# Sixteen slots instead of eight for expert weights, and a router with one copy of its logits and no transfers of gates and indices

## The chip, the cores and the metric

The kernel runs on one core of a Trainium2 chip. The metric is the device time of one execution in microseconds (us), the median over several runs. TensorE does the matrix products, VectorE (DVE in the rows) and ScalarE (ACT) the elementwise work, GpSimd (POOL) a few helpers and the gathers, SyncE (SP) issues the loads of weights. All data is float32.

## The reference

One token sequence of 512 tokens and 1024 features passes two blocks. The change touches the end of the first block: a mix (two branches and an output product), a router, and a mixture of 16 experts in which each expert chooses its 64 tokens.

```python
def expert_choice_moe(h, w_router, w_gate, w_up, w_down):
    b_, length, _ = h.shape
    cap = EC_CAPACITY_FACTOR * length // N_EXPERTS
    aff = jax.nn.softmax((h @ w_router).astype(jnp.float32), axis=-1)
    gate, idx = lax.top_k(jnp.swapaxes(aff, 1, 2), cap)
    bidx = jnp.arange(b_)[:, None, None]
    xe = h[bidx, idx]
    hid = jax.nn.silu(jnp.einsum("becd,edf->becf", xe, w_gate)) * jnp.einsum("becd,edf->becf", xe, w_up)
    ye = jnp.einsum("becf,efd->becd", hid, w_down) * gate[..., None].astype(h.dtype)
    return jnp.zeros_like(h).at[bidx, idx].add(ye)
```

w_gate, w_up and w_down are 16 matrices of 1024 x 1024 each: 201 MB that are read once. The second block (another attention, a convolution, a feed-forward layer of width 4096) follows and needs the whole result.

## The kernel before, in words

Each engine has its own program, written out by hand in one function per engine (`pe`, `act`, `dve`, `pool`, `sync`), with a nested function for each stage: `mix`, `router`, `experts`, `second` and so on. The order within an engine is the order of the code; between engines there are only semaphores. A first silent pass over all programs numbers the signals, a second one emits the instructions.

**Weights.** `weight_units` lists every weight load in the order in which it is needed. SyncE issues them in this order (L2566 to L2570). The class `Ring` gives each unit a place in a ring of eight slots of 2048 words per partition (`NS = 8`), so 1024 KB a slot. Before a load, SyncE waits until the holder of the slot has been read (`W.before`, `W.free`). It is one queue: a load that waits holds back all later loads. Units of the mix take two slots each. A unit of the experts takes one: two of the eight rows-of-128 of one expert's matrix, `k == 2`. The experts' units come in the order pair p of experts, then gate, up, down, then `kq` 0 to 3, then the two experts `e2`: 24 units a pair, 192 in all.

**Mix and router.** The mix ends with eight output products, ("wo", 0) to ("wo", 7). The router (L711 on TensorE) then does this, each step waiting for the one before: norm on VectorE and ScalarE into `h2T`; logits with `wr`, eight products in two groups of four (L718), which leave partial sums in four bands of 16 rows at rows 0, 32, 64 and 96; VectorE copies the four bands to `mrow` (L2123); TensorE turns them; VectorE adds the bands, softmax follows; TensorE turns the result to one row per expert, `aff`; VectorE draws the top 64 of 512 in eight rounds (L2145 to L2150) and casts the indices to float32, `ifl` (L2152). Meanwhile TensorE turns `h2T` to token rows, ScalarE copies them to `h2k` (L1410) and stores them to the DRAM scratch `h2_scratch` (L1413, called h_scratch in the rows: the h2 store). Then gates `gv` and indices `ifl`, 16 experts x 64 places each, have to come to one row per place for a pair of experts: four small transfers on ScalarE's queue bring them to `gi8` (L1417), TensorE turns them (L738, L739), VectorE copies them to `giT` and `idx` (L2154, L2155). GpSimd gathers the 128 token rows of pair 0 into `xe` (L2534), after `idx` and after the landing of the h2 store.

**Experts.** For each pair TensorE does `pair_product` of gate (L760), the `scatter` of the pair before (L771), `pair_product` of up, the turns of the next gathered rows, the turns of the hidden values, and `pair_product` of down. After each `kq` the two units read are free. VectorE compares `iot`, the numbers 0 to 511, with the indices to build the scatter matrix `PT` (L2189). After pair 7, the last scatter makes the input of the second block.

## Time and profile before

| | us |
|---|---|
| median of 3 runs | 1996.23 (1995.18 to 2000.35) |
| profiled execution | 1997.07 |
| its span, first to last instruction | 1995.8 |
| TensorE busy | 1762.4 (88%) |
| VectorE busy | 806.3 (40%) |
| ScalarE busy | 560.6 (28%) |
| mean DMA rate over the span | 165 GB/s |

The span is cut into stretches: the mix ends at about 722 us, the router runs to about 772, the experts to about 1252, the second block follows. In the rows PE is TensorE's product, PEld its load of the stationary side, POOL GpSimd, SPq, ACTq and POOLq the issue of a transfer. PS is the product memory. "DMA share" is the mean busy share of the 16 DMA engines. A row of the chain gives start, duration and what ran or was waited for. In a timeline the bracket says how long the engine had been idle and who released it. A group xN is N instructions of one form that followed one another, and the time of such a group reaches from its first start to its last end.

### The profile page before, as it was taken

How to read it: one execution, taken by the hardware profiler on the slowest of the kernel's cores; microseconds unless marked ns; L12 is line 12 of the kernel's file. 1: busy time of each engine (PE TensorE's matmuls, PEld its weight loads, DVE VectorE, ACT ScalarE, POOL GpSimd, SP SyncE). 2: the span in 40 equal slices, each digit the busy share in tenths (PEclk: the TensorE clock that was granted, in tenths of full speed). 3: DMA queues.
4: the chain of work that ended last, by engine and by line, in shares of the span. 5: the costliest groups of instructions: out<-in, count | busy, mean ns of one | idle time of the engine just before them, and what ended most of it. 6: DMA issues, size and time to landing. Idle time of an engine off the chain costs nothing.

```text
span 1995.8 us, 20238 instructions
## 1 busy us (share of the span) xinstructions
PE 1762.4 (88%) x8121; PEld 1140.0 (57%) x8121; DVE 806.3 (40%) x1315; ACT 560.6 (28%) x983; POOL 123.1 (6%) x127
## 2 busy tenths in 40 slices
PE   5999899887999875788888888899888899999998
PEld 2656567556778652233323233487545578888786
DVE  2154754467433342011111011428466634444443
ACT  3134543554423230000000000332444342222221
POOL 0002111113000001000000000000100101100010
PEclk9999899888999987999999999999899799999999
DMA  8221201123511415999999999353300113222301
GB/s 300 91 64 48 80 22 64 42 91 121 169 61 73 168 43 220 421 421 421 421 421 422 421 421 420 139 165 87 127 1 1 43 52 118 84 85 88 123 1 43
DMA packets 92448, 329.38 MB, mean 165 GB/s; under 512 B 7492, under 2 KB 22724, under 8 KB 67780
## 3 DMA queue, kind: packets, MB, share of 16 engines
q1 hardware_dynamic: 85408, 315.80, 41.0%
q10 hardware_dynamic: 5604, 8.04, 1.2%
q0 software_dynamic: 1344, 4.25, 0.6%
q8 instruction: 65, 1.06, 0.2%
q14 instruction: 27, 0.22, 0.0%
HBM read 322.82 MB, written 4.19 MB: 164 GB/s over the span
## 4 chain that ended last, share of the span: by engine, by line
PE 67%; DMA 13%; DVE 11%; ACT 5%; issue 3%; ACTq 1%; SPq 0%; DVEq 0%
PE PS L645 20%; PE PS L760 9%; PE PS L991 8%; PE PS L388 7%; DMA ring<-in_w_exp_down_dram 6%; DMA ring<-in_w_exp_gate_dram 6%; PE PS L384 3%; PE PS L519 3%; PE PS L771 3%; PE PS L601 2%; PE PS L826 2%; PE PS L444 1%; PE PS L666 1%; PE PS L941 1%; PE PS L872 1%
## 5 line engine op out<-in xcount | busy, mean ns | idle before, releaser
L760 PE MATMUL PS<-ring,xeT 128*64 128x512 f32 x1024 | 232.0, 604 | 38.7 <-DMA ring<-in_w_exp_gate_dram 36.4
L1703 DVE TENSOR_TENSOR wR<-ring,wR 128x1024 fp32r<-128x1024 f32 (+2 forms) x134 | 151.3, 1130 | 238.0 <-ACT wR L1102 237.8
L1102 ACT CAST wR<-ring 128x1024 fp32r<-128x1024 f32 (+2 forms) x134 | 130.0, 971 | 212.6 <-PE PS L991 128.1
L760 PEld LDWEIGHTS PS<-ring,xeT 128*64 128x64 f32 x1024 | 77.4, 139 | 191.9 <-issue 185.5
L991 PE MATMUL PS<-wR,hR 128*128 128x512 f32 x768 | 177.8, 392 | 8.9 <-DVE tmp L2421 6.9
L645 PE MATMUL PS<-xR,wR 128*128 128x512 f32 x768 | 175.6, 389 | 0.0
L991 PEld LDWEIGHTS PS<-wR,hR 128*128 128x128 f32 x768 | 144.7, 189 | 42.0 <-DVE tmp L2421 9.6
L645 PEld LDWEIGHTS PS<-xR,wR 128*128 128x128 f32 x768 | 144.0, 188 | 30.3 <-issue 0.4
L760 PE MATMUL PS<-ring,hidT 128*64 128x512 f32 x512 | 116.7, 603 | 24.5 <-DMA ring<-in_w_exp_down_dram 18.6
L645 PE MATMUL PS<-hR,wR 128*128 128x512 f32 x528 | 130.0, 404 | 9.2 <-DVE hR L2402 3.7
L645 PEld LDWEIGHTS PS<-hR,wR 128*128 128x128 f32 x528 | 100.6, 192 | 37.4 <-issue 10.5
L645 PE MATMUL PS<-hR1h,wR 128*128 128x512 f32 x320 | 106.7, 405 | 8.3 <-DVE hR1m L2080 7.4
L760 PEld LDWEIGHTS PS<-ring,hidT 128*64 128x64 f32 x512 | 38.3, 138 | 97.7 <-issue 89.9
L1433 ACT ACTIVATE hid<-PS 128x1024 f32<-128x1024 f32 x8 | 8.2, 1024 | 275.4 <-PE PS L760 275.4
L645 PEld LDWEIGHTS PS<-hR1h,wR 128*128 128x128 f32 x320 | 60.8, 190 | 25.5 <-DVE hR1m L2080 7.8
L2175 DVE TENSOR_TENSOR hid<-hid,PS 128x1024 f32<-128x1024 f32 x8 | 9.8, 1220 | 159.4 <-ACT hid L1433 159.4
L2187 DVE TENSOR_SCALAR ye<-PS,giT 128x512 f32<-128x512 f32 x16 | 11.3, 746 | 151.6 <-PE PS L760 151.6
L601 PE MATMUL PS<-Y 128*128 128x64 f32 x448 | 60.1, 292 | 9.0 <-DVE SS L1986 6.7
L601 PEld LDWEIGHTS PS<-Y 128*128 128x128 f32 x448 | 58.4, 209 | 15.3 <-DVE SS L1986 8.4
L388 PE MATMUL PS<-hT,ring 128*128 128x256 f32 (+1 forms) x192 | 63.1, 486 | 2.9 <-DMA ring<-in_w_in_dram 2.9
L388 PE MATMUL PS<-ring,hT 128*128 128x256 f32 x288 | 63.2, 379 | 0.0
L771 PE MATMUL PS<-PT,ye 128*128 128x512 f32 x128 | 59.1, 608 | 2.1 <-DVE PT L2189 2.1
(416 smaller groups left out, 2516.1 us busy)
## 6 DMA issues: line engine op xcount, KB each, us to landing
ring<-in_w_exp_gate_dram SPq DMA_DIRECT2D x64, 1024.0 KB, 13.6
ring<-in_w_exp_up_dram SPq DMA_DIRECT2D x64, 1024.0 KB, 13.6
ring<-in_w_exp_down_dram SPq DMA_DIRECT2D x64, 1024.0 KB, 13.0
ring<-in_w_mod_dram SPq DMA_DIRECT2D x12, 2048.0 KB, 8.0
ring<-in_w_in_dram SPq DMA_DIRECT2D x11, 2048.0 KB, 11.3
ring<-in_w_up_dram SPq DMA_DIRECT2D x8, 2048.0 KB, 9.0
ring<-in_w_down_dram SPq DMA_DIRECT2D x8, 2048.0 KB, 7.9
ring<-in_w_in_dram SPq DMA_DIRECT2D x9, 1024.0 KB, 5.3
```

The costliest lines, as they stand in the source:

```text
L384: return T.transpose(dst, src, ident[0:k, 0:k])
L388: mm = T.matmul(dst, l, r, start=(i == 0), stop=(i == len(pairs) - 1))
L444: mm = T.matmul(b, hT[:, k, 256 + 128 * i:384 + 128 * i], w[:, k, :], start=(k == 0), stop=(k == 7))
L519: T.matmul(b[:, 0:512], wh[k], hT[:, k, 256:768], start=(k == 0), stop=(k == 7))
L601: mm = T.matmul(b[:, 64 * x:64 * x + 64].rearrange("p (b m) -> p b m", m=LEVELS[l]), yy, half, start=True, stop=True)
L645: mm = T.matmul(b, o[s][:, k, :], x(t, k), start=(k == ks[0] and j == 0), stop=(k == ks[-1] and j == 2))
L760: mm = T.matmul(b[es, ns], stat[:, 2 * kq + k, es], W.view(units[e2])[:, k, ns], start=(kq + k == 0), stop=(kq == 3 and k == 1))
L771: T.matmul(b, ye[:, p % 2, 128 * k:128 * k + 128], PT[:, p % 2, :], start=True, stop=True) \
L826: mm = T.matmul(bs[i][:, 0:cs.stop - cs.start], hR2[:, s, kk + k, 128 * i:128 * i + 128], o[t][:, k, :], start=(kk + k + j == 0), stop=(kk ...
L991: mm = T.matmul(down[m], uR[:, r % 2, s, k, 128 * i:128 * i + 128], o[t][:, 0, 512 * q:512 * q + 512], start=(k + j == 0), stop=(k == 3 an ...
L1102: A.copy(parts(wR, chunks, n)[0], W.view(unit)[:, ks, cs]).then_inc(act_hi.sem, act_hi.up(key))
L1703: V.tensor_tensor(lo, W.view(unit)[:, ks, cs], hi.bitcast(F32), ALU.subtract) \
```

## The change

It has three parts.

First, four "rooms" of two slots each are added to the ring: `room0` and `room1` in memory of the mix (free after the last output product), `room2` where `h2k` lies (free when the h2 store has landed), `room3` where `h2T` lies (free after the last turn into `h2k`). Expert units now go round sixteen places. All other units stay in the ring of eight. `iot` moves out of the way of room 3, and its load moves behind the h2 store.

Second, `wr` is widened from 16 to 32 columns, cleared by a memset before its load, so that the logits' partial sums fill all 128 rows, and one copy takes them all.

Third, the four transfers to `gi8` go. TensorE multiplies `gv` and `ifl` directly with every second column of the identity, which selects the even or odd experts and turns in one product; the result lands in the same layout.

```diff
--- before.py
+++ after.py
@@ -84,19 +84,25 @@
 
 
 
-    def __init__(self, tensor, sems, units):
+
+    def __init__(self, tensor, sems, units, more):
         self.tensor, self.sems, self.units = tensor, sems, units
+        self.places = [tensor[:, 2048 * i:2048 * i + 2048] for i in range(NS)] + [place for _, place in more]
         self.number = {u[0]: i for i, u in enumerate(units)}
         self.slots, self.value, self.before, self.free = [], [], [], {}
-        at, count, holder = 0, [0] * NS, [None] * NS
+        at, turn, count, holder = 0, 0, [0] * len(self.places), [None] * NS + [what for what, _ in more]
         whole = self.number["gate"]
         for i, (name, sources, k, n) in enumerate(units):
-            size, top = 1 if k * n <= 2048 and k <= 4 else 2, 4 if 4 <= i < whole else NS
-            at = 0 if at + size > top or i == whole else at
-            if i == whole:
-                holder[4:] = ["scan"] * 4
-            slots = list(range(at, at + size))
-            at += size
+            if k == 2:
+                slots = [(at + turn) % NS if turn < NS else turn]
+                turn = (turn + 1) % len(self.places)
+            else:
+                size, top = 1 if k * n <= 2048 and k <= 4 else 2, 4 if 4 <= i < whole else NS
+                at = 0 if at + size > top or i == whole else at
+                if i == whole:
+                    holder[4:NS] = ["scan"] * 4
+                slots = list(range(at, at + size))
+                at = (at + size) % NS if i > whole else at + size
             count[slots[0]] += 16 * len(sources)
             self.slots.append(slots)
             self.value.append(count[slots[0]])
@@ -107,8 +113,10 @@
     def view(self, name):
         i = self.number[name]
         _, _, k, n = self.units[i]
-        o = self.slots[i][0] * 2048
-        return self.tensor[:, o:o + k * n].rearrange("p (k n) -> p k n", k=k)
+        first = self.slots[i][0]
+        if len(self.slots[i]) == 1:
+            return self.places[first].rearrange("p (k n) -> p k n", k=k)
+        return self.tensor[:, 2048 * first:2048 * first + k * n].rearrange("p (k n) -> p k n", k=k)
 
     def ready(self, name):
         i = self.number[name]
@@ -228,7 +236,8 @@
     xk = Area(nc, KEEP, KEEP + 4096).take("xk", [128, 4, 1024])
     top = Area(nc, KEEP + 4096, HT)
     xT, sq, rinv = top.take("xT", [128, 8, 512]), top.take("sq", [128, 2, 512]), top.take("rinv", [128, 512])
-    uT, wr, iot = hT[:, :, 0:512], hT[:, 0, 512:640].rearrange("p (k n) -> p k n", k=8), hT[:, 1:3, 512:768]
+    uT, wr = hT[:, :, 0:512], hT[:, 0, 512:768].rearrange("p (k n) -> p k n", k=8)
+    iot = Area(nc, HT, HT + 512).take("iot", [128, 2, 256])
 
     m5 = Area(nc, DYN, DYN + 5216)
     xeT, xe = m5.take("xeT", [128, 8, 2, 128]), m5.take("xe", [128, 1024])
@@ -241,7 +250,7 @@
     hid, hidT = m6.take("hid", [128, 8, 128]), m6.take("hidT", [128, 8, 128])
     aff, gv = m6.take("aff", [16, 512]), m6.take("gv", [16, 64])
     iu, ifl = m6.take("iu", [16, 64], U32), m6.take("ifl", [16, 64])
-    gi8, idx = m6.take("gi8", [8, 2, 128]), m6.take("idx", [128, 8], U32)
+    idx = m6.take("idx", [128, 8], U32)
     h2k = Area(nc, KEEP, KEEP + 4096).take("h2k", [128, 4, 1024])
     h2T = hT[:, 0:8, 0:512]
 
@@ -315,7 +324,11 @@
         return PS[:, 512 * b:512 * (b + n)]
 
 
-    W = Ring(ring, [sem(f"w_slot{i}") for i in range(NS)], weight_units(d))
+    rooms = [Area(nc, *ends).take(name, [128, 2, 2048]) for name, ends in
+             (("room0", (DYN + 5216, DYN + 9312)), ("room1", (DYN + 9312, DYN + 13408)), ("room2", (KEEP, KEEP + 4096)),
+              ("room3", (HT + 512, HT + 4608)))]
+    W = Ring(ring, [sem(f"w_slot{i}") for i in range(2 * NS)], weight_units(d),
+             [(what, room[:, i, :]) for what, room in zip(("mixed", "mixed", "h2k", "h2T"), rooms) for i in range(2)])
     signals = {}
 
     def signal(name):
@@ -335,7 +348,7 @@
     act_ffn, dve_ffn, pool_ffn, pe_ffn = (signal(n) for n in ("act_ffn", "dve_ffn", "pool_ffn", "pe_ffn"))
     s_ident, s_rows, s_rows2, s_gb, s_masks = sem("s_ident"), sem("s_rows"), sem("s_rows2"), sem("s_gb"), sem("s_masks")
     s_x, s_rope, s_wr, s_iot, s_x2 = (sem(n) for n in ("s_x", "s_rope", "s_wr", "s_iot", "s_x2"))
-    s_h2, s_gi, s_ga, s_sh, s_k2, s_out = (sem(n) for n in ("s_h2", "s_gi", "s_ga", "s_sh", "s_k2", "s_out"))
+    s_h2, s_ga, s_sh, s_k2, s_out = (sem(n) for n in ("s_h2", "s_ga", "s_sh", "s_k2", "s_out"))
 
 
     def col_chunks(name, unit, n_tiles, tiles_of_unit, nk=8):
@@ -715,7 +728,7 @@
             for k in range(8):
                 r = 32 * (k % 4)
                 T.wait_ge(*act_moe["h2T", k])
-                mm = T.matmul(b[r:r + 16, :], wr[:, k, :], h2T[:, k, :], start=(k < 4), stop=(k >= 4))
+                mm = T.matmul(b[r:r + 32, :], wr[:, k, :], h2T[:, k, :], start=(k < 4), stop=(k >= 4))
             mm.then_inc(pe_moe.sem, pe_moe.up("logit"))
             b = every.take(T, "logitT", dve_moe["logitT"])
             T.wait_ge(*dve_moe["logit"])
@@ -734,9 +747,12 @@
                         mm = turn(b[:, 128 * k:128 * k + 128], h2T[:, 4 * q + k, 128 * i:128 * i + 128])
                     mm.then_inc(pe_moe.sem, pe_moe.up(("h2k", i, q)))
             b = every.take(T, "gi", dve_moe["idx"])
-            T.wait_ge(s_gi, 64)
-            turn(b[:, 0:8], gi8[:, 0, :], 8)
-            turn(b[:, 8:16], gi8[:, 1, :], 8).then_inc(pe_moe.sem, pe_moe.up("gi"))
+            T.wait_ge(*dve_moe["topk"])
+            for n, src in enumerate((gv, ifl)):
+                for e2 in range(2):
+                    mm = T.matmul(b[64 * e2:64 * e2 + 64, 8 * n:8 * n + 8], src, ident[0:16, e2:16:2],
+                                  start=True, stop=True)
+            mm.then_inc(pe_moe.sem, pe_moe.up("gi"))
 
         def experts():
             def expert_in(p):
@@ -1032,7 +1048,9 @@
             pass
         W.free["scan"] = pe_scan["o", 3, 2]
         mix()
+        W.free["mixed"] = pe_mm[("wo", 7), 0]
         router()
+        W.free["h2T"], W.free["h2k"] = pe_moe["h2k", 3, 1], (s_h2, 16)
         experts()
         second()
         select()
@@ -1350,9 +1368,8 @@
                             A.copy(xT[:, k, :], bank(("xT", k))).then_inc(s.sem, s.up(("xT", k)))
                     if br == 0 and t == 7:
                         A.wait_ge(*dve_mix["hR", 7])
-                        A.dma_start(wr, d["w_router"].rearrange("(k p) n -> p k n", p=128)).then_inc(s_wr, 16)
-                        A.dma_start(iot, d["k_iota"].rearrange("(a b) -> a b", a=2).partition_broadcast(128)) \
-                            .then_inc(s_iot, 16)
+                        A.wait_ge(*dve_mix["wr0"])
+                        A.dma_start(wr[:, :, 0:16], d["w_router"].rearrange("(k p) n -> p k n", p=128)).then_inc(s_wr, 16)
                         A.wait_ge(*pe_mm[key, 0])
                         for k in range(4):
                             A.copy(aR[0][:, k], oattT[:, k, :]).then_inc(s.sem, s.up(("a2", k)))
@@ -1411,10 +1428,7 @@
                         .then_inc(s.sem, s.up(("h2k", i, q)))
             A.wait_ge(*s.last)
             A.dma_start(h2d.rearrange("(t p) n -> p t n", p=128), h2k).then_inc(s_h2, 16)
-            A.wait_ge(*dve_moe["topk"])
-            for e2 in range(2):
-                for n, src in enumerate((gv, ifl)):
-                    A.dma_start(gi8[:, n, 64 * e2:64 * e2 + 64], src[e2:16:2, :]).then_inc(s_gi, 16)
+            A.dma_start(iot, d["k_iota"].rearrange("(a b) -> a b", a=2).partition_broadcast(128)).then_inc(s_iot, 16)
 
         def experts():
             s = act_moe
@@ -2087,6 +2101,7 @@
                                            ALU.add).then_inc(s.sem, s.up(("y", t)))
 
             sub_lo(wRg, mix_chunks, 5)
+            V.memset(wr, 0.0).then_inc(s.sem, s.up("wr0"))
             for h in range(2):
                 gate(h)
                 gated(h)
@@ -2119,9 +2134,7 @@
                 V.scalar_tensor_tensor(h2T[:, k, :], xT[:, k, :], AB[:, 0, k:k + 1], rinv, ALU.mult, ALU.mult) \
                     .then_inc(s.sem, s.up(("h2T", k)))
             V.wait_ge(*pe_moe["logit"])
-            for c in range(4):
-                t = V.tensor_copy(mrow[32 * c:32 * c + 16, :], bank("logit")[32 * c:32 * c + 16, 0:512])
-            t.then_inc(s.sem, s.up("logit"))
+            V.tensor_copy(mrow, bank("logit")[:, 0:512]).then_inc(s.sem, s.up("logit"))
             V.wait_ge(*pe_moe["logitT"])
             V.tensor_reduce(lgt, bank("logitT")[:, 0:512].rearrange("p (i c x) -> p i x c", i=4, c=4)[:, :, 0:16, :], AX,
                             ALU.add).then_inc(s.sem, s.up("logitT"))
```

How SyncE's program changes, from the last load of the mix to pair 1. Before, with the semaphore that each group waits for:

```order
L2570 DMA ring<-in_w_out_dram 128x8x512 [waits dve_lo] x2
L2570 DMA ring<-in_w_exp_gate_dram 128x2048 [waits dve_lo] x8
L2570 DMA ring<-in_w_exp_up_dram 128x2048 [waits pe_moe] x8
L2570 DMA ring<-in_w_exp_down_dram 128x2048 [waits pe_moe] x8
L2570 DMA ring<-in_w_exp_gate_dram 128x2048 [waits pe_moe] x8
```

Now (room_174 to room_177 are rooms 0 to 3):

```order
L2583 DMA ring<-in_w_out_dram 128x8x512 [waits dve_lo] x2
L2583 DMA ring<-in_w_exp_gate_dram 128x2048 [waits dve_lo] x8
L2583 DMA room_174<-in_w_exp_up_dram 128x2048 [waits pe_mm] x2
L2583 DMA room_175<-in_w_exp_up_dram 128x2048 [waits pe_mm] x2
L2583 DMA room_176<-in_w_exp_up_dram 128x2048 [waits s_h2] x2
L2583 DMA room_177<-in_w_exp_up_dram 128x2048 [waits pe_moe] x2
L2583 DMA ring<-in_w_exp_down_dram 128x2048 [waits pe_moe] x8
L2583 DMA room_174<-in_w_exp_gate_dram 128x2048 [waits pe_moe] x2
```

The up units of pair 0 no longer wait for the gate products (pe_moe) but for the end of the mix (pe_mm), for the h2 store (s_h2), and for the turns of `h2T`. The down units wait for the gate products instead.

TensorE's program at the end of the router, from the last turns of `h2T` to the first gathered rows. Before:

```order
L384 MATMUL PS<-ident,hT 128x128 [waits dve_moe]
L384 MATMUL PS<-ident,hT 128x128 x3
L384 MATMUL PS<-ident,gi_134 128x8 [waits s_gi,act_moe]
L384 MATMUL PS<-ident,gi_134 128x8
L384 MATMUL PS<-ident,xe 128x128 [waits act_moe,s_ga]
```

Now:

```order
L397 MATMUL PS<-ident,hT 128x128 [waits dve_moe]
L397 MATMUL PS<-ident,hT 128x128 x3
L753 MATMUL PS<-ident,gv 64x8 [waits dve_moe,act_moe]
L753 MATMUL PS<-ident,gv 64x8
L753 MATMUL PS<-ident,ifl 64x8 x2
```

The two turns that waited for transfers (s_gi) have become four products that wait for VectorE's top-k alone (dve_moe).

## Rows read from the trace of the kernel before

**Rows 1.** Busy time by stretch; the first line names the columns.
```profile
core 0: us, PE busy (x) PEld busy (x) DVE busy (x) ACT busy (x) POOL busy (x), PEclk, DMA share, GB/s
723.00:750.00 27.00, 14.21 (x59) 8.02 (x58) 17.54 (x37) 14.53 (x22) 0.00 (x0) 0.81 0.03 11
755.00:778.00 23.00, 8.11 (x26) 3.61 (x28) 5.29 (x14) 2.45 (x3) 5.68 (x11) 0.52 0.17 46
778.00:783.00 5.00, 5.00 (x26) 1.68 (x24) 0.00 (x0) 0.00 (x0) 0.00 (x0) 1.00 0.72 257
783.00:1238.00 455.00, 389.98 (x1677) 141.77 (x1674) 70.16 (x93) 24.30 (x38) 5.63 (x6) 0.99 1.01 421
846.00:907.00 61.00, 52.23 (x228) 18.97 (x224) 9.67 (x13) 3.17 (x5) 0.94 (x1) 1.00 1.01 421
1253.00:1258.00 5.00, 3.75 (x5) 1.32 (x6) 2.12 (x5) 1.24 (x2) 0.00 (x0) 0.70 1.06 381
```

**Rows 2.** Chain that ended last, expert stage (start us, us, what).
```profile
903.74 3.65 PE PS L760 x16
...
1208.38 3.65 PE PS L760 x16
...
1248.54 3.67 PE PS L760 x16
```

**Rows 3.** Who waited for whom, 846 to 1248 us (us in total, times, longest).
```profile
PE PS L760 <- DMA ring<-in_w_exp_gate_dram: 31.3, 23, 2.5
...
PE PS L760 <- DMA ring<-in_w_exp_down_dram: 14.1, 12, 1.5
```

**Rows 4.** Timeline of the router (start us, us, engine line, what, idle before).
```profile
735.20 2.79 DVE L2123 COPY mrow<-PS 16x512 f32<-16x512 f32 x4 [1.88 <-PE PS L718]
...
740.52 0.22 DVE L2138 TENSOR_TENSOR lgt<-lgt,lst 128x64 f32<-128x64 f32 x1
740.86 0.54 PEld L384 LDWEIGHTS PS<-ident,lgt 128*16 128x16 f32 x4 [2.34 <-issue]
...
748.41 0.38 ACTq L1413 DMA_DIRECT2D h_scratch<-h2k  x1
...
760.11 0.18 DVE L2152 CAST ifl<-iu 16x64 f32<-16x64 uint32 x1
```

**Rows 5.** The same view, from the index transfers to the first expert product.
```profile
764.26 0.28 PEld L384 LDWEIGHTS PS<-ident,gi 8*128 8x128 f32 x2 [16.84 <-issue]
...
764.67 0.17 DVE L2154 COPY giT<-PS 128x16 f32<-128x16 f32 x1 [4.38 <-PE PS L384]
...
765.20 1.03 POOL L2534 DMA_INDIRECT xe<-h_scratch,idx  x1 [271.04 <-DVE idx L2155]
...
769.56 1.97 PE L384 MATMUL PS<-ident,xe 128*128 128x128 f32 x8 [4.93 <-DMA xe<-h_scratch,idx]
...
772.21 23.24 PE L760 MATMUL PS<-ring,xeT 128*64 128x512 f32 x96 [0.68 <-ACT xeT L1425]
...
778.33 11.10 SPq L2570 DMA_DIRECT2D ring<-in_w_exp_up_dram  x8
```

**Rows 6.** Line of the copy of a full 128x512 product.
```profile
L1713 DVE COPY mrow<-PS x4: 680/690/692, 24.7 to 36.4; 128x512 f32<-128x512 f32 x4
```

**Rows 7.** Line of the h2 store: landing.
```profile
DMA to landing us min/median/max: 6.4/6.4/6.4
```

**Rows 8.** Line of the gather, 760 to 770 us, the queues idle: landing.
```profile
DMA to landing us min/median/max: 4.3/4.3/4.3
```

**Rows 9.** The same line after 800 us, six gathers beside the weight stream: landing.
```profile
DMA to landing us min/median/max: 8.3/8.5/9.5
```

**Rows 10.** DMA issues on the page: KB each and us to landing.
```profile
ring<-in_w_exp_gate_dram SPq DMA_DIRECT2D x64, 1024.0 KB, 13.6
```

**Rows 11.** Timeline of the vector engine at the head of the mix.
```profile
520.89 1.23 DVE L1703 TENSOR_TENSOR wRg<-ring,wRg 128x1024 fp32r<-128x1024 f32 x1 [5.00 <-ACT wRg L1102]
```

**Rows 12.** Line of a memset of 128x512.
```profile
L1731 DVE MEMSET mrow<- x1: 485/485/485, 1.3 to 1.3; 128x512 f32 x1
```

## The prediction

> **What bounds the kernel now.** The profiled execution took 1997.07 us, 0.84 above the median of the three runs shown; its span is 1995.8. I read three views, in this order. First the busy time by stretch: where are the DMA engines full, and where is TensorE? From 783 to 1238 the DMA share is 1.01 at 421 GB/s, while TensorE is busy for 390 of 455 us. The reader is to see that in the expert stage the share of TensorE (86%) looks high, but the thing that has no gap is the weight stream. From 723 to 750 and from 755 to 778, the router and the first gather, the stream is nearly silent: 11 and 46 GB/s [rows 1]. Second the chain of waits, which says what sets the period of the stage: five pairs of experts from 903.74 to 1208.38, so 60.93 us a pair [rows 2]. A pair is 24 units of 1024 KB [rows 10], 25.17 MB, which need 59.8 us at 421 GB/s; one gather of 512 KB adds 1.2. That is the whole period. TensorE has work for 52.23 us of such a pair [rows 1], and the waits table confirms the order: over six and a half pairs TensorE waited 31.3 + 14.1 = 45.4 us for gate and down weights [rows 3], about 7 a pair. Third the timeline between the mix and the first pair. With eight slots, the eight gate units of pair 0 lie ready before the router starts, and the next unit is not issued until TensorE has freed a slot, at 778.33 [rows 5]. From there 184 units follow without a gap; the last lets TensorE go at 1248.54 [rows 2]. So the end of the stage is the moment the stream resumes plus the bytes still missing at that moment. All later work hangs on it.
>
> **Eight more slots.** They take eight of the 184 units out of the stream after the resumption and put them into the silent stretch. Eight units are 8.39 MB; at 421 GB/s that is 19.9 us. This counts only if all eight are there in time. Four go to the rooms of the mix, free when the last product of the mix is done (723); the first stretch of rows 1 is empty enough: 4.19 MB are 10 us, over by about 735, before the h2 store. The other four are issued in order behind a wait for the landing of the h2 store. That store is issued at 748.41 [rows 4], lands 6.4 later [rows 7], and all of it comes 2.1 earlier (below): 752.7. A burst on an idle queue begins to move late: between 778 and 783 the mean was 257 GB/s [rows 1], 1.29 MB, 3.05 us of full rate, so data began near 779.95, 1.6 after the issue at 778.33. Hence the four rooms fill from 754.3 to 764.3. The stream resumes near 774 (below), so there are 10 us to spare, and all eight count.
>
> Does a later wait give it back? A slot is reused 16 units on instead of 8, so the queue waits less than before at every unit. TensorE would need about 52.2 us of work plus some hand-overs, say 54, a pair: 768 + 8 × 54 = 1200 for the end of the last product, against 1252.2 − 24.0 = 1228.2 for the end that the stream sets (now 1248.54 + 3.67 [rows 2]). The stream still ends last, with 28 us of margin. SP is in order: what stands behind the room loads on it are the later weights alone, which had to wait for slots anyway.
>
> **Router logits in one copy.** Four copies of 16 rows take 2.79 us in all [rows 4]. One copy of 128 x 512 takes 0.69 [rows 6]. The price follows the columns, not the rows, and the chain logits, copy, turns, softmax, top-k has nothing beside it: −2.1 us. The logit products become 32 wide instead of 16; their moving side is the same 512 columns, so nothing. The memset that clears the padding covers 256 columns; 512 take 0.485 [rows 12], so 0.25, and VectorE has 5.00 us idle before its next piece of work there [rows 11]: nothing; without that cover it would cost the 0.25.
>
> **Gates and indices by products.** Now the cast of the indices ends at 760.29 [rows 4], four small transfers follow on the ACT queue, the last issued at 762.47, and TensorE starts at 764.26 [rows 5]: 3.97 us. In their place stands a hand-over from VectorE to TensorE. Such a one took 0.12 (740.74 to 740.86) [rows 4]: −3.85. Two turns of eight rows took 0.41 up to the copy behind them (764.26 to 764.67) [rows 5]; the four products are twice as many: +0.4, between 0 and +0.8. I take −3.4 for this part, −5.5 with the copy. The first gather moves from 765.20 to 759.7.
>
> **The iota load** leaves the mix (it was off the path) and stands behind the h2 store on the ACT queue. It is 256 KB, 0.6 us of the stream's rate; VectorE asks for it only after the first gate product, near 785. Nothing.
>
> **What is late next: the first gather.** It used to run on idle queues, 4.3 us to landing [rows 8]. At 759.7 the second four room loads still have 4.6 us to run. The six later gathers, beside a full stream, took 8.3 to 9.5, median 8.5 [rows 9]. So its cost is between 0 and +4.2. It carries 0.52 MB, 1.25 us at full rate. Were it served only after the rooms, it would be over at 764.3 + 1.25 and a few tenths, 765.9; alone it would land at 764.0. I take +1.4, nearer the low end since its neighbour stops at 764.3, while in rows 9 the stream never stops.
> The Trainium skill (DMA: Bandwidth & Descriptors, Queues, rings and completion order) says that each DMA engine goes round between the queues at packet granularity, and (Issuing engines are not separate DMA queues) that transfers of all issuing engines share the same 16 engines. This speaks against the change: the gather cannot pass the room loads. By that rule it shares half and half while they last, an estimate of one more gather's transfer time, +1.25 us, and the sum would differ by 0.15 us. The loaded gathers of the trace agree in direction (8.5 against 4.3).
>
> **Sum.** From the landing of the gather to the first expert product nothing changes: 769.56 to 772.21 [rows 5]. That product starts 5.5 − 1.4 = 4.1 earlier, at 768.1, and the stream resumes 6.1 after it, as now, at 774.2. The stage ends 19.9 + 4.1 = 24.0 us earlier, and nothing behind it changes: second-block weights use the same slots and get them no later. 1997.07 − 24.0 = 1973.1; from the median, 0.84 lower, 1972.2. This last I forecast. Its own bounds: gather free of charge and products free of charge, 19.9 + 5.9 = 25.8, 1970.4; gather at its full +4.2 and products at +0.8, 19.9 + 0.9 = 20.8, 1975.4.
>
> **Rivals.**
> A, half the rooms fill too late (the h2 store lands late beside the iota load, or the four loads behind it hold the gather back as long as they hold each other). For it: everything behind that one wait is in order on SP. Against: 10 us to spare. Only four units count: 10 + 4.1 gives 1982.1.
> B, TensorE becomes the bound. For it: it is busy 52.23 of 61 us and each product waits for one of another engine. Against: rows 3 name DMA before it, for 7 us a pair. It decides from 57.5 us a pair (1228.2 − 768 over eight); at 59 the last product ends at 768 + 472 = 1240, and the gain is 12.2 us: 1984.0.
> C, slower than before: with up to 16 loads outstanding the stream itself runs slower over the whole stage. The one place in the profile where a full share of DMA moves less is 1253 to 1258, with four large loads queued: 381 GB/s at a share of 1.06 [rows 1]. After the resumption 176 units remain, 184.6 MB: 438.4 us at 421, 484.4 at 381. That is +46.0 against −24.0: 2018.2. It decides from 399 GB/s down. Against it: those loads have rows of 2 KB, the expert loads 8 KB, and they ran at 421 for 455 us with up to eight outstanding.
> D, the change does not do what it says: the stage is paced by both sides together, so a head start is lost again within the first pairs, and only the 4.1 us of the router stay: 1992.1. Against it: no gap in the DMA share.
>
> **How the numbers follow.** The forecast within its own bounds has 0.78; A and what lies between it and the forecast 0.08; B 0.04; D 0.03; C 0.03; the other 0.04 is a gain above 26 us. The range for 8 in 10 takes in the forecast's bounds and about 1.5 us on either side for the spread between runs, and reaches toward A: 1969 to 1979. What this kernel's measurement tells from no change is about 0.3%, 6 us. Faster by more: all but C, D and the tail of B, 0.94. Within 0.3%: D and that tail, 0.03. Slower: C, 0.03.
>
> **What would show it.** In the profile after: a DMA share near 1 for 10 us from 723 and for 10 us from about 754; the first gather issued near 759.7 and landing between 4.3 and 6.5 us later; the first expert product near 768, the next weight issue near 774; the period of the late pairs still 60.9 with TensorE waiting for DMA, but in pairs 0 to 3 hardly at all; the last expert product near 1224.5, and everything behind it shifted as a block. The prediction is wrong if the DMA share has gaps between 780 and 1224, if the early pairs take longer than 57 us though no weight is late, or if the gather lands after 768.

## The result, and the profile after

The changed kernel took 1970.64 us (median of 4 runs, 1966.23 to 1973.28) against 1997.1 for the kernel before: a ratio of 0.9864, 95% interval 0.9839 to 0.9888. The forecast was 1972.2, the range 1969 to 1979. A second series gave 1971.64 against 2001.85, ratio 0.9857 (0.9829 to 0.9884). So the gain between medians was 26.5 us in the first series and 30.2 in the second; the forecast was 24.0.

The profiled execution after took 1966.23, which is 30.8 us less than the one before, more than the medians differ. To see what of this is the change, I measure from two marks that exist in both programs: the first instruction of the router on VectorE, right behind the last product of the mix, and VectorE's first read of the last expert product. The timeline of VectorE before has them here:

```profile
723.04 0.16 DVE L2112 SCALAR_TENSOR_TENSOR AB<-modc,colA 128x8 f32<-128x8 f32 x1
...
1252.31 1.41 DVE L2187 TENSOR_SCALAR ye<-PS,giT 128x512 f32<-128x512 f32 x2 [18.05 <-PE PS L760]
```

The same view after, with the router between them:

```profile
718.78 0.16 DVE L2127 SCALAR_TENSOR_TENSOR AB<-modc,colA 128x8 f32<-128x8 f32 x1
...
731.00 0.69 DVE L2137 COPY mrow<-PS 128x512 f32<-128x512 f32 x1 [1.95 <-PE PS L731]
...
753.80 0.18 DVE L2165 CAST ifl<-iu 16x64 f32<-16x64 uint32 x1
...
1223.54 1.41 DVE L2200 TENSOR_SCALAR ye<-PS,giT 128x512 f32<-128x512 f32 x2 [17.79 <-PE PS L776]
```

Between the marks lie 529.3 us before and 504.8 after: 24.5 less, where 24.0 were forecast. The other 6.4 us lie outside: 4.3 ahead of the first mark and 2.1 behind the second. They come back in the section on the experiments, with what they do to the times of the whole.

The busy time by stretch after the change answers to [rows 1]:

```profile
core 0: us, PE busy (x) PEld busy (x) DVE busy (x) ACT busy (x) POOL busy (x), PEclk, DMA share, GB/s
720.00:730.00 10.00, 5.30 (x16) 1.41 (x16) 5.39 (x8) 8.70 (x12) 0.00 (x0) 0.66 0.95 402
730.00:742.00 12.00, 8.43 (x45) 6.86 (x41) 8.25 (x21) 4.58 (x9) 0.00 (x0) 0.71 0.01 1
742.00:750.00 8.00, 0.00 (x0) 0.00 (x0) 7.64 (x18) 0.16 (x1) 0.00 (x0) 0.60 0.78 295
750.00:762.00 12.00, 0.59 (x8) 0.53 (x8) 4.03 (x11) 0.00 (x0) 4.65 (x10) 0.50 0.98 391
763.00:772.00 9.00, 8.33 (x26) 3.29 (x27) 0.00 (x0) 2.45 (x3) 1.03 (x1) 0.56 0.21 58
772.00:777.00 5.00, 5.00 (x26) 1.68 (x24) 0.00 (x0) 0.00 (x0) 0.00 (x0) 1.00 0.82 297
783.00:1205.00 422.00, 376.21 (x1628) 136.22 (x1624) 69.44 (x93) 22.36 (x36) 5.63 (x6) 1.00 1.01 424
```

From 720 to 730 the stream moves 402 GB/s, where there was nothing: rooms 0 and 1. From 730 to 742 it is silent; then come the h2 store and rooms 2 and 3, until 762. Then the first pair starts, and the stream resumes; from 783 on it has no gap, at 424 GB/s instead of 421.

The end of the router, in the timeline after, answers to [rows 4, 5]:

```profile
754.13 0.38 PE L753 MATMUL PS<-ident,gv 16*64 16x8 f32 x4 [12.69 <-DVE ifl L2165]
...
755.29 1.03 POOL L2547 DMA_INDIRECT xe<-h_scratch,idx  x1 [265.80 <-DVE idx L2168]
...
762.73 1.97 PE L397 MATMUL PS<-ident,xe 128*128 128x128 f32 x8 [8.01 <-DMA xe<-h_scratch,idx]
...
765.38 16.71 PE L776 MATMUL PS<-ring,xeT 128*64 128x512 f32 x64 [0.67 <-ACT xeT L1439]
...
771.83 11.11 SPq L2583 DMA_DIRECT2D ring<-in_w_exp_down_dram  x8
```

VectorE casts the indices until 753.98; the products start 0.15 later. The gather is issued 1.31 after the cast's end, where it was 4.91. But the gathered rows come 7.44 us after the gather's issue, where it was 4.36: the landing took

```profile
DMA to landing us min/median/max: 7.4/7.4/7.4
```

against 4.3 before [rows 8]. The first expert product starts 46.6 us after the first mark (before: 49.2) and the next weight load is issued at 53.1 (before: 55.3).

The chain of waits shows the late pairs still paced by the stream. It follows gate products that waited for a load; the first of them stands in pair 2, and the last down product, 1207.69, no longer waits in the chain:

```profile
877.01 3.65 PE PS L776 x16
...
1179.88 3.65 PE PS L776 x16
...
1207.69 15.76 PE PS L776 x64
```

Five pairs now take 302.87 us, 60.57 a pair, against 60.93 [rows 2]. The waits table from 846 to 1224 us has these rows for TensorE and the weights, 37.4 us in all over 378 us, against 45.4 over 402 [rows 3]:

```profile
PE PS L776 <- DMA room<-in_w_exp_gate_dram: 14.6, 11, 2.2
PE PS L776 <- DMA ring<-in_w_exp_gate_dram: 12.4, 10, 1.6
...
PE PS L776 <- DMA ring<-in_w_exp_down_dram: 5.6, 5, 1.3
...
PE PS L776 <- DMA room<-in_w_exp_down_dram: 4.8, 4, 1.4
```

And a load is now issued about 27 us ahead of its landing instead of 14 [rows 10], since TensorE frees sixteen places:

```profile
ring<-in_w_exp_gate_dram SPq DMA_DIRECT2D x32, 1024.0 KB, 26.9
```

### The profile page after: what moved, and what is told of

The parts are those of the page before. It is cut to its first block, busy times and chain, and to the rows that moved or that the text cites. A ratio compares the mean times of both kernels' runs of the same rounds, so it can differ in the third digit from the quotient of the medians.

```text
span 1964.9 us, 20245 instructions
## 1 busy us (share of the span) xinstructions
PE 1758.2 (89%) x8127; PEld 1137.8 (58%) x8127; DVE 803.8 (41%) x1313; ACT 560.5 (29%) x983; POOL 123.1 (6%) x127
## 4 chain that ended last, share of the span: by engine, by line
PE 71%; DMA 10%; DVE 10%; ACT 5%; issue 3%; ACTq 0%; SPq 0%; DVEq 0%
PE PS L658 21%; PE PS L776 11%; PE PS L1007 9%; PE PS L401 7%; DMA ring<-in_w_exp_gate_dram 4%; DMA room<-in_w_exp_gate_dram 4%; PE PS L397 3%; PE PS L532 3%; PE PS L787 3%; PE PS L614 2%; PE PS L842 2%; PE PS L457 1%; PE PS L679 1%; DMA ring<-in_w_in_dram 1%; PE PS L957 1%
## 5 line engine op out<-in xcount | busy, mean ns | idle before, releaser
L776 PE MATMUL PS<-room,xeT 128*64 128x512 f32 x512 | 115.0, 602 | 14.6 <-DMA room<-in_w_exp_gate_dram 14.6
L776 PE MATMUL PS<-ring,xeT 128*64 128x512 f32 x512 | 116.1, 607 | 13.1 <-DMA ring<-in_w_exp_gate_dram 12.4
L658 PEld LDWEIGHTS PS<-hR,wR 128*128 128x128 f32 x528 | 102.0, 195 | 36.2 <-issue 9.4
L776 PEld LDWEIGHTS PS<-room,xeT 128*64 128x64 f32 x512 | 38.4, 138 | 90.5 <-issue 88.2
L776 PEld LDWEIGHTS PS<-ring,xeT 128*64 128x64 f32 x512 | 38.1, 139 | 90.0 <-issue 85.9
L776 PE MATMUL PS<-room,hidT 128*64 128x512 f32 x256 | 58.5, 610 | 7.7 <-DMA room<-in_w_exp_down_dram 4.8
L776 PE MATMUL PS<-ring,hidT 128*64 128x512 f32 x256 | 56.9, 595 | 8.6 <-DMA ring<-in_w_exp_down_dram 5.6
## 6 DMA issues: line engine op xcount, KB each, us to landing
room<-in_w_exp_up_dram SPq DMA_DIRECT2D x32, 1024.0 KB, 26.5
```

Source lines behind the costliest of these rows:

```text
L658: mm = T.matmul(b, o[s][:, k, :], x(t, k), start=(k == ks[0] and j == 0), stop=(k == ks[-1] and j == 2))
L776: mm = T.matmul(b[es, ns], stat[:, 2 * kq + k, es], W.view(units[e2])[:, k, ns], start=(kq + k == 0), stop=(kq == 3 and k == 1))
```

## The experiments

Eleven variants were run, and the changed kernel a second time. All times in this table come from the timeline of each one's profile, counted from the first mark. "First product" is the first expert product, "next load" the first weight load issued after it, "last product" the second mark, "behind" the rest of the span. GB/s is the mean of 800 to 1190 us. Each row is one profile. The two profiles of the changed kernel differ by 1.3 us at the next load and by 1.5 at the last product, but only by 0.2 in the stretch between the two; differences of that size carry nothing.

| kernel | first product | next load | last product | behind | GB/s |
|---|---|---|---|---|---|
| before | 49.2 | 55.3 | 529.3 | 743.5 | 421 |
| changed | 46.6 | 53.1 | 504.8 | 741.4 | 424 |
| changed, again | 45.6 | 51.8 | 503.2 | 741.4 | 424 |
| slots_only | 52.9 | 58.8 | 510.3 | 741.0 | 424 |
| router_only | 43.2 | 48.8 | 522.6 | 749.2 | 421 |
| rooms_mix | 43.2 | 48.8 | 512.6 | 742.2 | 421 |
| no_head_start | 43.5 | 49.8 | 521.0 | 749.1 | 424 |
| gather_first | 43.1 | 48.8 | 502.9 | 748.8 | 424 |
| h2t_first | 46.6 | 52.3 | 503.7 | 741.1 | 424 |
| rooms_router | 45.8 | 51.9 | 512.1 | 749.8 | 424 |
| places_14 | 43.1 | 48.8 | 506.0 | 741.9 | 423 |
| sixteen_short | 43.6 | 50.0 | 521.0 | 749.2 | 423 |
| base_128 | 45.7 | 51.9 | 499.9 | 741.4 | 427 |
| base_64 | 44.6 | 50.3 | 504.6 | 741.4 | 421 |

The expectations of the first four variants speak of the time of the whole, and there the gains came out larger than between the marks for three of them. By their ratios, applied to the median of before in that series (2001.31), the gains are 23.6 us for slots_only (20.0 to 27.2), 6.4 for router_only (2.8 to 10.0), 22.0 for rooms_mix (17.6 to 26.2) and 11.4 for no_head_start (7.6 to 15.0); between the marks they are 19.0, 6.7, 16.7 and 8.3. Part of this lies, by all appearance, in the reference: the one profile of before is an execution of 1997.07 us, 4.2 below that median. I judge the theories by the marks, where the change acts, and give the figures of the whole where they would say otherwise.

**slots_only.** The sixteen places with the router of before, but for the iota load, which stays behind the h2 store. Its edit puts back the narrow `wr`, the four copies, the four transfers and the turns (the `...` stands for lines left out):

```diff
-            T.wait_ge(*dve_moe["topk"])
...
+            T.wait_ge(s_gi, 64)
+            turn(b[:, 0:8], gi8[:, 0, :], 8)
+            turn(b[:, 8:16], gi8[:, 1, :], 8).then_inc(pe_moe.sem, pe_moe.up("gi"))
```

> The sixteen places alone; the router has its four copies and its four transfers of gates and indices again. Theory (what counts is the bytes loaded in the silent stretch of the router): eight units at 421 to 424 GB/s, 19.8 to 19.9 us, less about 1 us by which the first gather, issued 10 us after the room loads instead of 7, is held up beside them; 18.5 to 21.5 us below the kernel before. Rival (TensorE and the stream pace each other and the head start is lost): under 8 us.

Measured: 1976.18, ratio 0.9882 (0.9864 to 0.99); 19.0 us less between the marks, in the expected band of 18.5 to 21.5, and 23.6 of the whole, above it, with an interval (20.0 to 27.2) that still takes in half of the band. The gather was not held up, it landed after 4.4 us. The small transfers ahead of it were, as the timeline shows:

```profile
758.74 0.63 ACTq L1431 DMA_DIRECT2D gi<-ifl  x1
...
764.19 0.28 PEld L397 LDWEIGHTS PS<-ident,gi 8*128 8x128 f32 x2 [20.54 <-issue]
764.22 0.35 PE L397 MATMUL PS<-ident,gi 8*128 8x8 f32 x2 [20.33 <-DMA gi<-ifl]
...
765.13 1.04 POOL L2548 DMA_INDIRECT xe<-h_scratch,idx  x1 [274.72 <-DVE idx L2169]
```

The cast ended at 756.56, so the way over the transfers to TensorE's first load took 7.63 us, where it took 3.97 on idle queues. The loads of rooms 2 and 3 ran beside them: they were issued from 751.79 on, and the last landed at 764.40. The expectation named the wrong victim for the right cause.

**router_only.** The new router on eight slots:

```diff
-    W = Ring(ring, [sem(f"w_slot{i}") for i in range(2 * NS)], weight_units(d),
-             [(what, room[:, i, :]) for what, room in zip(("mixed", "mixed", "h2k", "h2T"), rooms) for i in range(2)])
+    W = Ring(ring, [sem(f"w_slot{i}") for i in range(NS)], weight_units(d), [])
```

> The router alone (one copy, products with the identity, iota load behind the h2 store) on eight slots. Theory: the first gather is issued 5.6 us earlier from the end of the mix and lands in 4.3 us since nothing is beside it, so the stream resumes 5.5 us earlier and the whole is 5 to 6 us below the kernel before. Rival (the top-k and the h2 store hide it): 0 to 2 us.

Measured: 1993.94, ratio 0.9968 (0.995 to 0.9986); 6.7 us less between the marks, next load 6.5 earlier. The router's part is on the path; it is 0.7 to 1.7 us larger than expected, which is about the spread between two profiles. Alone, the two parts give 19.0 and 6.7; together 24.5 and 26.1.

**rooms_mix.** Twelve places:

```diff
-    W = Ring(ring, [sem(f"w_slot{i}") for i in range(2 * NS)], weight_units(d),
-             [(what, room[:, i, :]) for what, room in zip(("mixed", "mixed", "h2k", "h2T"), rooms) for i in range(2)])
+    W = Ring(ring, [sem(f"w_slot{i}") for i in range(12)], weight_units(d),
+             [(what, room[:, i, :]) for what, room in zip(("mixed", "mixed"), rooms) for i in range(2)])
```

> Twelve places: only the two rooms in the memory of the mix, with the new router. Theory: four units, 9.9 us, and the router's full 5.5 us, since no load stands beside the gather: 15 to 16.5 us below the kernel before, landing of the first gather 4.3 us. Rival (more than eight slots give more than their bytes, by never letting the queue run short): within 3 us of the changed kernel, over 21 us.

Measured: 1978.07, ratio 0.989 (0.9869 to 0.9912); 16.7 less between the marks, just above the expected 15 to 16.5, and the first gather:

```profile
DMA to landing us min/median/max: 4.4/4.4/4.4
```

Against router_only the stage is 10.1 us shorter: four units at 421 GB/s are 9.96, and 10.0 of the 10.1 lie between the next load and the last product. The rival wanted over 21 and within 3 us of the changed kernel. The whole gained 22.0, which alone would pass the first half, but the changed kernel gained 27.2 and 28.6 by the same reckoning. Between the marks, rooms_mix is 7.8 and 9.3 us behind the changed kernel.

**no_head_start.** The first load of each room waits for the first gate product:

```diff
-        W.free["mixed"] = pe_mm[("wo", 7), 0]
         router()
-        W.free["h2T"], W.free["h2k"] = pe_moe["h2k", 3, 1], (s_h2, 16)
         experts()
+        W.free["mixed"] = W.free["h2T"] = W.free["h2k"] = pe_moe["gate", 0, 0]
```

> All sixteen places, but the first load of every room waits until the first gate product has been read, as the ninth unit did before; so nothing is loaded in the silent stretch. Theory: only the router's 5.5 us remain, 5 to 6.5 us below the kernel before. Rival (depth of the buffer, and a stream that runs at 424 instead of 421 GB/s with 16 loads outstanding): 8 us or more below.

Measured: 1987.83, ratio 0.9943 (0.9925 to 0.9962); 8.3 less between the marks. So 16 to 18 us of the changed kernel's 24.5 and 26.1 go with the head start. But 8.3, and the 11.4 of the whole still more, is the rival's figure, and one half of the rival was right: the stream ran at 424 GB/s, and from the next load to the last product it took 471.1 us where before and router_only took 474.0 and 473.8. That is a gain of 2.6 to 2.8 us with no byte moved ahead.

**after_again, gather_first, h2t_first.** The first is the changed kernel once more. In gather_first rooms 2 and 3 wait for the landing of the first gather (`s_ga`), in h2t_first room 3 is filled before room 2. The edits:

```diff
-        W.free["h2T"], W.free["h2k"] = pe_moe["h2k", 3, 1], (s_h2, 16)
+        W.free["h2T"], W.free["h2k"] = pe_moe["h2k", 3, 1], (s_ga, 16)
```

in gather_first, and in h2t_first

```diff
+    order = (0, 1, 3, 2)
     W = Ring(ring, [sem(f"w_slot{i}") for i in range(2 * NS)], weight_units(d),
-             [(what, room[:, i, :]) for what, room in zip(("mixed", "mixed", "h2k", "h2T"), rooms) for i in range(2)])
+             [(("mixed", "mixed", "h2k", "h2T")[r], rooms[r][:, i, :]) for r in order for i in range(2)])
```

> The changed kernel once more, beside the two variants of this call. From the stage marks of its first profile (first weight issue of the stream 2.2 us earlier after the mix, 22.3 us less from there to the last expert product) the change is worth 24.5 us; its first profiled run was 30.8 us below that of before, of which 4.3 us came ahead of the end of the mix and 2.1 us behind the experts, where no instruction on the path was changed. If these 6.4 us are spread between runs, this run shows 24 to 26 us in the stage and other figures outside it; if they are of the change, the same 4.3 and 2.1 come back.

Measured: 26.1 in the stage; ahead of the first mark 2.2 us less than before instead of 4.3, behind the second 2.1 again. Over all kernels of the table the first mark lies between 718.8 and 726.6 us though the work ahead of it is the same but for a memset and one load; and "behind" falls in two groups, 741.0 to 743.5 and 748.8 to 749.8, which I can tie to no edit: no_head_start and router_only are in the second, rooms_mix and base_128 in the first. The groups part in 24 us of the second block's attention, 270 us behind the second mark: up to 266 us behind it VectorE's instructions run level in after_again and gather_first (0.1 us apart), and at 290 us they are 7.2 apart; the other four profiles of the second group part there too. After_again, then gather_first (columns as above):

```profile
1494.00:1518.00 24.00, 20.75 (x126) 12.84 (x124) 15.94 (x56) 10.42 (x46) 0.00 (x0) 0.81 0.00 1
```

```profile
1495.50:1519.50 24.00, 24.00 (x99) 13.22 (x97) 10.24 (x32) 7.39 (x30) 0.00 (x0) 0.54 0.00 1
```

The granted clock is 0.81 in one and 0.54 in the other, so mostly at 1.2 instead of 2.4 GHz, for the same instructions. So most of the 2 to 6 us outside the marks is spread between executions or follows the point in time, not the change's work. Of the 2.1 us behind the second mark this is not shown, for they came back, and before has one profile alone; slots_only has them without the new router (741.0), and router_only, on eight slots, lies among the others of its group (749.2). What decides the group stays open. A kernel's median moves by some microseconds with how many of its executions fall in the second group, and only profiled executions show theirs.

> As the changed kernel, but rooms 2 and 3 are first filled only when the first gather has landed. Theory (the gather was held up by the room loads, 7.4 us instead of 4.3): the gather lands in 4.3 us, the first expert product and the resumption come 3 us earlier; the stream is then without a gap from the landing on, four room units first, and ends about 2 us earlier than in the changed kernel. Rival (the 7.4 us have another cause, as the h2 store or the iota load): landing unchanged, and the time 3 us or more above the changed kernel, since four units start 9 us later.

Measured: 1975.58, ratio 0.9869 (0.9838 to 0.99). The gather's rows came 4.36 us after its issue, the first product and the next load came 2.6 and 2.9 earlier than in after_again. So the room loads were what held the gather; places_14, with two loads behind the h2 store instead of four, had the same 4.36. Yet the last product came only 0.3 earlier than in after_again and 1.9 earlier than in the first profile, since the four loads of rooms 2 and 3 began only when the gather had landed. The expected 2 us were not confirmed in the whole: its median is 3.9 us above after_again's in the same series, and its profile is in the group with the slower rest.

> As the changed kernel, but room 3 (free when the last turn is done) is filled before room 2 (free when the h2 store has landed). Theory: two units come beside the h2 store and delay its landing by 2 to 5 us, two are left beside the gather, whose landing falls from 7.4 to about 6 us; together -1.5 to +0.5 us against the changed kernel. Rival (the gather waits for the h2 store in the end): first gather issued later than 38 us after the end of the mix and the time above the changed kernel.

Measured: 1970.21, ratio 0.9851 (0.9821 to 0.988), no difference from the changed kernel. The gather was issued 36.2 us after the mark, as in the changed kernel (36.5 and 36.1), and its rows came 7.7 us later, no better. The rival's late issue did not come, nor did the gain. The reason is in the h2 store: beside the two loads of room 3 it took

```profile
DMA to landing us min/median/max: 13.1/13.1/13.1
```

instead of 7.1, more than the 2 to 5 us of delay that I expected. The two loads of room 2 wait for it, were issued at 755.81, 0.8 us ahead of the gather, and so stood beside it whole.

**rooms_router, places_14, sixteen_short** ask why the stream runs at 424. The first two change the list of rooms as rooms_mix does, to ("h2k", "h2T") and to the first three; the third adds to no_head_start

```diff
+            if k == 2 and units[i - 8][2] == 2:
+                self.before[-1].append(units[i - 8][0])
```

> Twelve places again, but with the rooms of the router (h2k, h2T) instead of those of the mix. In the runs so far the stream moved 421 GB/s with 8 or 12 places and 424 with 16. Theory D (depth of the queue): 421 here, since it has 12 places. Theory P (place: rooms 2 and 3 take the writes faster): 423 or 424. In time: four units at 421, 9.9 us in the stage, and the first gather held up as in the changed kernel: 513 to 515 us from the end of the mix to the last expert product, against 529.3 before.

> Fourteen places: rooms 0, 1 and 2. Theory D: between 421 and 424 GB/s or already 424, landing near 27 us; theory P: 422 to 423. Six units, 14.9 us, and the router: 507 to 509 us from the end of the mix to the last expert product.

> The sixteen places without a head start, and each expert load waits in addition until the unit eight before it has been read: the same places are written in turn, but no more than eight units are ahead. Theory D: 421 GB/s, landing near 13 us, 522 to 524 us from the end of the mix to the last expert product, as with the router alone (522.6). Theory P: 424 GB/s and 520 to 521 us, as without the head start (521.0).

Measured, with one execution each but for rooms_mix: rooms_mix, rooms_router, places_14 and sixteen_short moved in 800 to 1190 us

```profile
800.00:1190.00 390.00, 336.68 (x1452) 122.25 (x1450) 59.84 (x81) 19.04 (x30) 4.68 (x5) 1.00 1.01 421
```

```profile
800.00:1190.00 390.00, 336.91 (x1465) 122.83 (x1464) 60.56 (x82) 21.18 (x34) 5.65 (x6) 1.00 1.01 424
```

```profile
800.00:1190.00 390.00, 339.32 (x1471) 122.85 (x1468) 59.91 (x82) 20.05 (x31) 4.68 (x5) 1.00 1.01 423
```

```profile
800.00:1190.00 390.00, 333.09 (x1436) 121.41 (x1433) 60.42 (x82) 21.11 (x34) 5.63 (x6) 1.00 1.01 423
```

Depth is out: the same twelve places' worth of queue gives 421 or 424 by which rooms they are, and with at most eight units ahead, landing in

```profile
room<-in_w_exp_gate_dram SPq DMA_DIRECT2D x32, 1024.0 KB, 14.0
```

the stream still reached 423, and the stage took 521.0 us, theory P's value. (Rooms_router and places_14 took 512.1 and 506.0 between the marks, each about 1 us below its expected band.) What rooms 2 and 3 have that the others have not is their address: from the numbers in the code, the ring and rooms 0 and 1 start 128 bytes behind a multiple of 256 in each partition (16512 = 64 × 256 + 128), rooms 2 and 3 on a multiple.

**base_128, base_64** move all memory:

```diff
-BASE = 16512
+BASE = 16640
...
-              ("room3", (HT + 512, HT + 4608)))]
+              ("room3", (HT + 544, HT + 4640)))]
```

and, for base_64, `BASE = 16576` alone.

> The changed kernel with all its memory moved up by 128 bytes in each partition (the address of the first word from 16512 to 16640) and room 3 by 128 bytes more. Then 14 of the 16 places (the ring, rooms 0, 1 and 3) start at a multiple of 256 bytes and room 2 does not; in the changed kernel only rooms 2 and 3 do. Theory A (the start of the destination row): loads into aligned places run at x, into others at 421 GB/s; 425 with 4 aligned places of 12, 424 with 4 of 16 and 423 with 2 of 14 all give x near 433, so here 431 GB/s, and the 176 units take 7 us less: 495 to 498 us from the end of the mix to the last expert product against 503 to 505. Theory B (the region of memory, or the number of distinct regions): 424 GB/s and 503 to 505 us.

> The changed kernel with all its memory moved up by 64 bytes, so that no place of the expert weights starts at a multiple of 256 bytes, nor of 128. Theory A: 421 GB/s at all places and 505.5 to 508 us from the end of the mix to the last expert product. Theory B: 424 GB/s and 503 to 505 us.

Measured: base_64 and base_128 in the same stretch

```profile
800.00:1190.00 390.00, 342.15 (x1488) 124.52 (x1486) 60.92 (x82) 21.20 (x34) 5.65 (x6) 1.00 1.01 421
```

```profile
800.00:1190.00 390.00, 345.98 (x1503) 126.38 (x1502) 65.20 (x88) 22.20 (x35) 5.64 (x6) 1.00 1.01 427
```

From the next load to the last product base_64 took 454.3 us, the changed kernel 451.7 and 451.5, base_128 448.1. Moving everything by 64 bytes takes the gain away, which no theory of regions gives; moving it by 128 gives more. Between the marks the verdict is less clean: the 504.6 of base_64 lies in theory B's band (503 to 505), because its rooms 2 and 3 were loaded from 28.2 us after the mark on (30.5 in the changed kernel), the gather landed after 5.9 us, and the next load came at 50.3. The 499.9 of base_128 lies between the two bands.

The size was half of what I expected, 427 instead of 431, and the traces tell why. Each row of 8192 bytes of an expert load is one packet in the DMA records, 24576 in all, with its duration. Sorted by start and counted off by 128, one unit after the other, from unit 32 on, and averaged by place (0 to 7 the ring, 8 to 15 the rooms), their means are 314 ns at every place in before, rooms_mix and base_64 (312 to 315) and 309 to 310 at every place in base_128. In the changed kernel they are 313 to 314 at places 4 to 11, 309 at the last three of the four places of rooms 2 and 3, and also 309 at the next two, in the ring, which are not on a multiple; the rest lie between. Places_14 has two aligned places, and about four fast units; rooms_router has four, and about seven. So a fast row saves 1.6%, and two to three units behind an aligned room are fast with it. I had put the whole gain down to the aligned places alone, and so took their rate too high. The same holds in base_128, whose room 2 is not aligned and shows no slower rows. Why the effect reaches on is open.

Base_128 took 1965.19 us, ratio 0.9815 (0.9797 to 0.9833) to before, the lowest median of all kernels run. It beats the kernel before; against the changed kernel, measured in other series (0.9839 to 0.9888, 0.9829 to 0.9884), the second interval touches its own, so that the difference of the whole is likely and not shown. Between the marks it is 3.3 and 4.8 us shorter than the changed kernel. The Trainium skill (DMA: Bandwidth & Descriptors, How a descriptor splits into AXI transactions) says that a descriptor is cut at multiples of 256 bytes and that one which starts between them needs a partial piece more. For rows of 8192 bytes that is 33 pieces instead of 32, an estimate of 3% from the Trainium skill, or 260 beats instead of 256 by its count of beats, 1.6%, for a start 128 bytes behind a multiple. The runs agree in sign, with 1.4% in the rate for base_128 (427 against 421) and 1.6% in the rows. But the section does not say that its split holds for the address written to, base_64, with starts 192 and 64 bytes behind, has the same 314 ns as before, and neither count gives the fast units behind an aligned room. That the start address matters is shown; the mechanism is not.

## Why the prediction was right, point by point

**The bound.** The stream ends the stage, and the stage shortens by what is moved into the silent stretch. Shown: four units gave 10.1 us (rooms_mix against router_only), and without the head start 16 us of the gain were gone. Rival D is out by this, and rival B by the 37.4 us that TensorE still waited for weights. Rival C is out: with 27 us from issue to landing the stream was not slower. Rival A is out: all four late loads were done by 762.1, 9.7 us before the next load was due.

**Eight units, 19.9 us.** From the next load to the last product the changed kernel took 22.3 and 22.5 us less. Of these about 19.7 are bytes and 2.7 a faster stream (no_head_start), by where the new rooms lie. This term was 2.5 us too small; nothing in my sum asked where a load is written to.

**The copy, −2.1, and the products, −3.4.** In router_only the gather was issued 6.1 us earlier: 2.5 up to the cast, 3.6 from there. The four products took 0.63 us up to the copy behind them, the two turns 0.41: +0.2, where I had +0.4. With rooms 2 and 3 loading, the old transfers took another 3.7 us (slots_only). I looked for what the room loads would do to the gather, and not for what they would have done to the small transfers that went.

**The gather, +1.4.** This is the term that was mis-sized: measured +3.1 and +2.5, within the bounds of 0 and +4.2. Two things add up. The h2 store took 7.1 us to land instead of 6.4, with the iota load right behind it on its queue (7.3 in router_only, where no room load follows), and so the loads behind it were issued at 749.3, 30.5 us after the mark, where my sum had 29.7. And I took a value between the gather alone and the gather served last; it was served nearly last. Its first packet moved 4.2 us after its issue, where it was 1.7 on idle queues, and its last ended at 762.40, the loads' last at 762.08, 43.3 us after the mark; the rows were there at 43.95. Sharing half and half from the issue on, which I had estimated at +1.25, is not what the trace shows. What it costs in the end is less, though, as gather_first shows: 0.3 to 1.9 us, because the loads that delay it are themselves the stream.

**The sum.** 2.2 and 3.5 us from the router's side (forecast 4.1), 22.3 and 22.5 from the stream (19.9): 24.5 and 26.1 (24.0). The mechanism held; that the sum came so near is in part luck, by two misses of opposite sign. There is luck in the whole as well: I worked from a median of 1996.23, the series gave 1997.1, and its gain of 26.5 us lies above the 25.8 that were my bound, the 30.2 of the second series further still. What the whole gained beyond the stage is the part outside the marks, for which my sum had nothing. And TensorE waited for weights again from pair 2 on, where I had pairs 0 to 3 nearly free of waits.

## What to carry to other kernels

When a stage is bound by a stream that has no gap, look for the nearest stretch in which the stream is silent, and for memory that is dead there: each unit of buffer filled then is worth its transfer time, and the buffer's later depth gave nothing here. Before filling such a stretch, list the small transfers on its path; four of them stretched by 3.7 us here beside large loads, and work that can be done by an engine should leave the queues. And look at the start address of each row that is written.

## What the runs showed of the hardware

Rows of 8 KB written to places that start on a multiple of 256 bytes moved faster than others: 421 GB/s with no place aligned (four kernels), 423 with 2 of 14, 423 to 424 with 4 of 16 or 4 of 12, 427 with 14 of 16. A row took 309 ns instead of 314, at aligned places and for two to three loads of 1 MB behind them. Where the places were alike, the number of loads outstanding made no difference to the rate: 421 with 8 and with 12, 424 with 16 and 423 with 8. A round of four transfers of 2 KB took 3.97 us from the end of the work before it to TensorE on idle queues and 7.63 beside large loads. A gather of 512 KB landed after 4.3 us on idle queues and after 6.8 and 7.4 when it was issued with 2.1 and 2.3 MB of loads still to move on another queue. The granted clock in one stretch of the second block was 0.81 in one kernel and 0.54 in another with the same instructions there, and 7.2 us of the time were lost there.
